# A hybrid attention and expert-lookup layer: the query-key product of each attention head contracts over 64 partitions instead of 128

## The chip, the core and the metric

The kernel runs as one program on one core of a Trainium2 chip. The metric is the device time of one execution in microseconds (us), taken as the median of several runs. All arithmetic is in float32.

## The reference, cut to what matters

One layer processes a prompt of 1024 tokens and a decoding sample of 64 tokens. A projection feeds two groups of heads, A and B. Then come an output projection, an expert lookup and a small gated tail:

```python
a = rmsnorm(h, norm_mix); z = a @ w_in
# group A: 4 heads x 128, gated DeltaNet in chunks. group B: 8 heads x 64, forgetting attention
s = einsum('bqhd,bkhd->bhqk', q, k) * 64 ** -0.5           # DH_B = 64
s = s + c_q[..., None] - c[:, :, None, :]                  # c: running sum of log f, per head
s = where(pos_q[:, None] >= pos_k[None, :], s, -inf)
o = einsum('bhqk,bkhd->bqhd', softmax(s), v)
h = h + concat(A, B) @ w_out
# expert lookup: 8 heads pick 16 of 16384 experts each, so 128 rows of u and 128 rows of v per token
h = h + sum_k softmax(score)_k * gelu(u[e_k] . x) * v[e_k]
```

Only the first product of the attention, queries times keys, is what the change touches.

## The kernel before, in words

**Tiles and steps.** The 1024 prompt tokens are nine tiles with the sample: tiles 0 to 7 of 128 tokens, and the sample as tile 8 (`LAST`). The program is 12 steps. Step `s` runs the front of tile `s` (projections, convolution, DeltaNet, attention, output projection, choice of experts), the u rows of tile `s-1`, the v rows of the tiles `s-2` and `s-3`, and the tail of tile `s-3`. Steps 1 and on have 68 slots. `plan_front` (L130) writes by hand which stage has a part in which slot; every engine walks the same plan in the same order (`walker`, L466), so the order on each engine is fixed, and only semaphores tie the engines together.

**Expert rows.** From slot 4 on each slot has two u rows and two v rows. Every row is one indirect DMA of 128 x 1024 floats (512 KB) that POOL issues (L674) into a ring of 10 buffers. A u buffer is used up by a dot product on DVE (L1664). A v buffer is used up by TensorE (`weighted`, L1204, matmul L1218): the stationary operand has 32 columns and goes to a 32-partition stripe of the output bank, so two tokens use different column stripes. POOL issues into a buffer only when its last user has signalled `consumed`.

**Attention.** In tile `i` a head sees `blocks_of(i)` blocks of 128 keys: i+1 of them for the prompt, two for the sample. Up to four blocks (512 columns) are one half, so tiles 0 to 3 and 8 have one half per head and tiles 4 to 7 have two. `fox_s` (L1129, slots 22 to 38) makes one half of the scores in `BB[0]` with two matmuls that accumulate: L1141, queries times keys, and L1142, which adds the running sums of log f (stationary `faux`, moving `aux`, both 128 partitions, mostly zeros). DVE then reduces the half with its mask (L1510) and frees the bank; ScalarE takes the exponential (L853); `fox_o` (L1146) transposes the probabilities (L1155) and multiplies them with the values (L1166). Between these stand the matmuls of the DeltaNet's triangular inverse (L1071, L1078, L1080) and the L1218 of the slot.

**Where the 64 partitions are.** The query projection leaves two heads per 128 partitions: head 2m on partitions 0 to 63, head 2m+1 on 64 to 127. ScalarE writes each head into its own `[128, 128]` slice of `fqT` (L773), on the partitions that it came on. The other 64 partitions of the slice are zeros from one memset at the start (L552). `kTc[:, h // 2, :]` holds the keys of both heads of a pair, on the same partitions. So L1141 contracts over 128 partitions, and the zeros of the queries drop the neighbour's keys.

**Records.** The trace shows a float32 matmul as two records, each a weight load (LDWEIGHTS, PEld) and a MATMUL (PE). A form such as `128*32` is the stationary operand's partitions times its columns.

Of the kernel before, what the change touches and what calls it, by code (L numbers as in the profile page):

```python
# [17 lines left out]
HA, HB, DHB = 4, 8, 64  # L18
# [57 lines left out]
def halves_of(i):  # L76
    return -(-blocks_of(i) // 4)
# [199 lines left out]
def build(nc, t, out):  # L277
    ctx = ExitStack()
    with ctx:
        def sb(name, shape, dt=F32):  # L280
            return ctx.enter_context(nc.sbuf_tensor(name, shape, dt))
# [36 lines left out]
        fqT = sb("fqT", [P, HB, P])  # L318
        kTc = sb("kTc", [P, HB // 2, SEQ])
# [79 lines left out]
        BB = [psum(f"bbank{g}", 512) for g in range(2)]  # L399
# [12 lines left out]
        def till(name, i, v=None):  # L412

            return S[name], at(name, i, v)
# [27 lines left out]
        def wait_out(eng, i, *pieces):  # L442

            for name in pieces:
                wait_piece(eng, PIECE_NO[i, name])
# [15 lines left out]
        def halves(i):  # L461

            n = blocks_of(i)
            return [range(4 * g, min(4 * g + 4, n)) for g in range(halves_of(i))]
# [112 lines left out]
        with nc.Block() as block:  # L577
# [348 lines left out]
            def _(pe):  # L926
# [202 lines left out]
                def fox_s(i, h):  # L1129
                    if h == 0:  # L1130
                        wait_out(pe, i, "fox_q0", "fox_q1")
                        pe.wait_ge(*till("aux_ready", i))
                    for g, own in enumerate(halves(i)):
                        m = halves_of(i) * h + g
                        if m == 0:
                            pe.wait_ge(*till("kT_done", i))
                        else:
                            pe.wait_ge(*till("s_red", i, m))
                        c = slice(P * own[0], P * own[-1] + P)
                        w = P * len(own)  # L1140
                        pe.matmul(BB[0][:, 0:w], fqT[:, h, :], kTc[:, h // 2, c], start=True, stop=False)  # L1141
                        pe.matmul(BB[0][:, 0:w], faux[:, h, :], aux[:, c], start=False, stop=True)\  # L1142
                            .then_inc(S["s_mm"], 1)
                        yield
# [84 lines left out]
                stages.update({f"conv{g}": (lambda i, g=g: conv(i, g)) for g in range(3)})  # L1229
                stages.update({f"inv{l}": (lambda i, l=l: inverse(i, l)) for l in range(LEVELS)})  # L1230
                stages.update({f"fox_s{h}": (lambda i, h=h: fox_s(i, h)) for h in range(HB)})
                stages.update({f"fox_o{h}": (lambda i, h=h: fox_o(i, h)) for h in range(HB)})
                stages.update({f"out{j}": (lambda i, j=j: out_proj(i, j)) for j in range(4)})
# [508 lines left out]
```

## Time and profile before

| | |
|---|---|
| median of 3 runs | 4056.99 us (4051.64 to 4060.16) |
| the profiled execution | 4062.07 us, span 4060.1 us |
| mean granted clock of TensorE | 0.874 of full speed |
| PE / DVE / POOL busy | 72% / 64% / 51% of the span |
| DMA | 1463 MB, 360 GB/s over the span |

The profiled execution is 2 us longer than its span, and 5 us longer than the median. Busy time of PE is modelled at its ends, so a busy PE is not PE at its peak; differences between start times are exact, and the text works with these.

### The profile page before, as it was taken

How to read it: one execution, taken by the hardware profiler on the slowest of the kernel's cores; microseconds unless marked ns; L12 is line 12 of the kernel's file. 1: busy time of each engine (PE TensorE's matmuls, PEld its weight loads, DVE VectorE, ACT ScalarE, POOL GpSimd, SP SyncE). 2: the span in 40 equal slices, each digit the busy share in tenths (PEclk: the TensorE clock that was granted, in tenths of full speed). 3: DMA queues.
4: the chain of work that ended last, by engine and by line, in shares of the span. 5: the costliest groups of instructions: out<-in, count | busy, mean ns of one | idle time of the engine just before them, and what ended most of it. 6: DMA issues, size and time to landing. Idle time of an engine off the chain costs nothing.

```text
span 4060.1 us, 42281 instructions
## 1 busy us (share of the span) xinstructions
PE 2913.4 (72%) x15157; PEld 1720.8 (42%) x15157; DVE 2582.4 (64%) x6198; ACT 564.5 (14%) x1106; POOL 2089.7 (51%) x2206
## 2 busy tenths in 40 slices
PE   6656627875887578876887589758885587566587
PEld 5656524443543354444545355435443353232122
DVE  3388885668666966687576856686564856495411
ACT  2112111101210021101110122012210121001000
POOL 0014435664566555755565546645563456546763
PEclk9778768987998899987999799879997799788899
DMA  6159959998999999999999999999999899999996
GB/s 200 54 215 369 349 206 412 410 410 339 413 411 410 372 383 412 406 404 351 413 388 413 349 413 375 403 346 411 390 343 326 325 413 409 350 346 399 410 407 262
DMA packets 390527, 1463.24 MB, mean 360 GB/s; under 512 B 64816, under 2 KB 67824, under 8 KB 355760
## 3 DMA queue, kind: packets, MB, share of 16 engines
q0 software_dynamic: 313344, 1140.99, 72.6%
q1 hardware_dynamic: 72112, 301.98, 18.9%
q10 hardware_dynamic: 4864, 17.57, 1.1%
q8 instruction: 122, 2.00, 0.2%
q14 instruction: 85, 0.70, 0.0%
HBM read 1446.15 MB, written 13.97 MB: 360 GB/s over the span
## 4 chain that ended last, share of the span: by engine, by line
PE 29%; DMA 28%; DVE 22%; POOL 11%; issue 8%; ACT 2%; DVEq 0%; ACTq 0%; POOLq 0%
DMA ring<-peer_v,idxT 23%; PE ybank L1218 11%; POOL ring L674 11%; DVE ring L1664 7%; PE abank L951 5%; PE abank L955 5%; DMA ring<-peer_u,idx 4%; DVE arena L1567 1%; DVE arena L1575 1%; DVE arena L1569 1%; DVE arena L1572 1%; DVE arena L1564 1%; PE bbank L1141 1%; PE bbank L1142 1%; PE bbank L1166 1%
## 5 line engine op out<-in xcount | busy, mean ns | idle before, releaser
L674 POOL DMA_INDIRECT ring<-peer_u,idx x1088 | 1038.2, 954 | 1374.9 <-PE ybank L1218 696.7
L1218 PE MATMUL ybank<-ring,vst 128*32 128x512 f32 x4352 | 1205.3, 688 | 612.1 <-DMA ring<-peer_v,idxT 598.4
L1664 DVE CUSTOM_DVE_ANT_0 ring<-ring,xn 128x1024 f32<-128x1024 f32 x1088 | 1298.9, 1217 | 504.7 <-DMA ring<-peer_u,idx 493.7
L674 POOL DMA_INDIRECT ring<-peer_v,idxT x1088 | 1042.6, 958 | 546.0 <-issue 258.7
L1218 PEld LDWEIGHTS ybank<-ring,vst 128*32 128x32 f32 x4352 | 251.0, 118 | 1288.4 <-issue 1280.8
L951 PEld LDWEIGHTS abank<-aT,wring 128*128 128x128 f32 x4608 | 544.9, 198 | 169.6 <-issue 154.3
L951 PE MATMUL abank<-aT,wring 128*128 128x128 f32 x4608 | 568.4, 284 | 63.3 <-issue 49.5
L955 PE MATMUL abank<-wring,aT 128*128 128x256 f32 (+1 forms) x1440 | 344.0, 396 | 12.2 <-DVEq L1326 6.8
L955 PEld LDWEIGHTS abank<-wring,aT 128*128 128x128 f32 x1440 | 278.2, 198 | 105.4 <-issue 60.0
L699 ACT ACTIVATE arena<-abank 128x256 f32<-128x256 f32 (+1 forms) x180 | 68.8, 383 | 1172.6 <-PE abank L951 898.5
L973 PE MATMUL bbank<-ident,arena 128*128 128x128 f32 x9 | 4.3, 474 | 246.8 <-DVE arena L1625 246.8
L955 PE MATMUL abank<-wring,arena 128*128 128x256 f32 (+2 forms) x648 | 173.8, 421 | 0.8 <-DVE arena L1270 0.8
L1653 DVE TENSOR_TENSOR vst<-wT,unit 128x128 f32<-128x128 f32 (+1 forms) x288 | 81.0, 282 | 123.2 <-PE ybank L1218 120.2
L955 PEld LDWEIGHTS abank<-wring,arena 128*128 128x128 f32 (+1 forms) x648 | 120.2, 192 | 57.4 <-issue 39.5
L1510 DVE CUSTOM_DVE_ANT_0 arena<-bbank,causal 128x512 f32<-128x512 f32 (+3 forms) x104 | 56.7, 545 | 125.7 <-PE bbank L1142 125.3
L1564 DVE MAX8 arena<-arena 128x8 f32<-128x128 f32 (+1 forms) x216 | 62.0, 328 | 111.1 <-ACT arena L891 108.9
L973 PEld LDWEIGHTS bbank<-ident,arena 128*128 128x128 f32 x9 | 1.6, 181 | 255.7 <-DVE arena L1625 255.7
L1664 DVE DVE_READ_ACCUMULATOR2_ANT dots<- 128x1 f32 x1088 | 89.1, 82 | 0.0
L1166 PEld LDWEIGHTS bbank<-vc,arena 128*128 128x128 f32 x608 | 74.7, 194 | 33.3 <-issue 25.9
L1141 PE MATMUL bbank<-kTc,fqT 128*128 128x512 f32 (+3 forms) x208 | 85.2, 492 | 0.6 <-DVE fst L1510 0.6
L1166 PE MATMUL bbank<-vc,arena 128*128 128x64 f32 x608 | 81.0, 278 | 5.2 <-ACT arena L862 5.2
L1142 PE MATMUL bbank<-aux,arena 128*128 128x512 f32 (+3 forms) x208 | 83.2, 482 | 0.0
(268 smaller groups left out, 2697.4 us busy)
## 6 DMA issues: line engine op xcount, KB each, us to landing
wring<-w_pieces SPq DMA_DIRECT2D x252, 1024.0 KB, 8.1
wring<-w_pieces SPq DMA_DIRECT2D x18, 1056.0 KB, 8.3
ring<-peer_u,idx POOLq DMA_INDIRECT x1088, 9.2
ring<-peer_v,idxT POOLq DMA_INDIRECT x1088, 9.3
wring<-w_pieces SPq DMA_DIRECT2D x18, 512.0 KB, 6.8
h_rows<-x ACTq DMA_DIRECT2D x8, 512.0 KB, 9.4
h<-h_rows ACTq DMA_DIRECT2D x8, 512.0 KB, 6.9
out_y_prompt<-arena ACTq DMA_DIRECT2D x8, 512.0 KB, 9.3
```

What stands on the lines that cost most here:

```text
L674: pool.indirect_dma_start(out=ring[:, r, :], out_offset=None, in_=t["peer_" + kind], in_offset=bass.IndirectOffsetOnAxis(ap=where, axis=0) ...
L699: last = act.activation(dst, src, func, scale=scale)
L951: last = pe.matmul(b[:, m * P:m * P + rows], wt[:, k, m * P:(m + 1) * P], actT[:, k, 0:rows], start=(k == 0), stop=(k == DK - 1))
L955: last = pe.matmul(b[0:rows, 0:w], actT[:, k, 0:rows], wt[:, k, :], start=(k == 0), stop=(k == k8 - 1))
L1141: pe.matmul(BB[0][:, 0:w], fqT[:, h, :], kTc[:, h // 2, c], start=True, stop=False)
L1142: pe.matmul(BB[0][:, 0:w], faux[:, h, :], aux[:, c], start=False, stop=True)\
L1166: last = pe.matmul(BB[1][:, 0:DHB], pts[:, m, :], vc[:, m, h * DHB:(h + 1) * DHB], start=(m == 0), stop=(m == n - 1))
L1218: last = pe.matmul(YB[g][QUAD * j:QUAD * j + QUAD, :], vst[:, slot, j, :], ring[:, r, 512 * g:512 * g + 512], start=(n // q == 0), stop=(n ...
L1510: v.tensor_tensor_reduce(out=pbuf[h % 2][:, c], in0=BB[0][:, 0:w], in1=mask, scale=1.0, scalar=NEG * 10, op0=ALU.add, op1=ALU.max, accum_o ...
L1564: last = v.max(vals[:, 0:8], values)
L1653: v.tensor_tensor(vst[:, n % VST, 0:q, :], bcast(columns, QUAD), over(unit[:, QUAD - 1 - m:2 * QUAD - 1 - m], q), ALU.mult)\
L1664: v.tensor_tensor_reduce(out=ring[:, r, :], in0=ring[:, r, :], in1=XN[:], scale=1.0, scalar=0.0, op0=ALU.mult, op1=ALU.add, accum_out=dots ...
```

## The change

The slice of partitions of head `h` is taken from both operands of L1141. The slice of an even head is 0 to 63, that of an odd head 64 to 127. The number of columns, the output, the accumulation with L1142, the semaphores and the memset of `fqT` stay as they are.

```diff
                         w = P * len(own)
-                        pe.matmul(BB[0][:, 0:w], fqT[:, h, :], kTc[:, h // 2, c], start=True, stop=False)
+                        o = DHB * (h % 2)
+                        pe.matmul(BB[0][:, 0:w], fqT[o:o + DHB, h, :], kTc[o:o + DHB, h // 2, c], start=True, stop=False)
                         pe.matmul(BB[0][:, 0:w], faux[:, h, :], aux[:, c], start=False, stop=True)\
```

## Rows read from the trace of the kernel before

**Rows 1.** The page: the span, and the chain that ended last by engine and line.
```profile
span 4060.1 us, 42281 instructions
PE 29%; DMA 28%; DVE 22%; POOL 11%; issue 8%; ACT 2%; DVEq 0%; ACTq 0%; POOLq 0%
DMA ring<-peer_v,idxT 23%; PE ybank L1218 11%; POOL ring L674 11%; DVE ring L1664 7%; PE abank L951 5%; PE abank L955 5%; DMA ring<-peer_u,idx 4%; DVE arena L1567 1%; DVE arena L1575 1%; DVE arena L1569 1%; DVE arena L1572 1%; DVE arena L1564 1%; PE bbank L1141 1%; PE bbank L1142 1%; PE bbank L1166 1%
```

**Rows 2.** Attention stages of tiles 0, 3, 4, 7: busy time, granted clock, DMA.
```profile
core 0: us, PE busy (x) PEld busy (x) DVE busy (x) ACT busy (x) POOL busy (x), PEclk, DMA share, GB/s
70.00:171.00 101.00, 67.55 (x397) 60.68 (x395) 41.02 (x95) 26.48 (x65) 0.00 (x0) 0.80 0.19 68
...
1142.00:1225.00 83.00, 73.46 (x380) 37.38 (x378) 56.82 (x112) 14.96 (x33) 57.94 (x61) 0.96 1.03 410
1572.00:1665.00 93.00, 82.08 (x453) 44.79 (x451) 65.51 (x148) 19.28 (x44) 61.89 (x67) 0.98 1.02 405
...
2877.00:2978.00 101.00, 95.00 (x488) 51.47 (x486) 62.54 (x134) 21.86 (x40) 59.42 (x64) 0.97 0.96 362
```

**Rows 3.** Chain of waits by line, stages of tiles 0, 4, 5, 6, 7, 8.
```profile
by line: PE abank L1071 8.5%; PE abank L951 7.3%; PE abank L1080 7.2%; PE abank L1078 7.0%; issue 4.8%; DVE arena L1424 3.8%; PE abank L955 3.4%; PE bbank L1166 3.1%; PE bbank L1141 2.5%; PE bbank L1142 2.4%; PE abank L1089 2.1%; PE abank L
...
by line: DMA ring<-peer_v,idxT 30.6%; PE ybank L1218 27.3%; POOL ring L674 10.1%; PE bbank L1141 6.8%; PE bbank L1142 6.7%; PE bbank L1166 6.0%; PE abank L1080 5.0%; PE abank L1071 4.7%; PE abank L1078 4.7%; issue 4.7%; PE bbank L1155 4.2%;
...
by line: DMA ring<-peer_v,idxT 29.2%; PE ybank L1218 28.5%; PE bbank L1166 8.4%; PE bbank L1141 8.0%; PE bbank L1142 8.0%; PE bbank L1155 5.4%; POOL ring L674 5.4%; PE abank L1080 4.8%; PE abank L1078 4.5%; PE abank L1071 4.5%; issue 3.4%; 
...
by line: DMA ring<-peer_v,idxT 29.1%; PE ybank L1218 26.0%; PE bbank L1166 9.6%; PE bbank L1141 9.1%; PE bbank L1142 9.1%; PE bbank L1155 5.9%; PE abank L1080 4.7%; PE abank L1078 4.4%; PE abank L1071 4.4%; POOL ring L674 2.8%; issue 2.5%; 
...
by line: PE ybank L1218 29.1%; DMA ring<-peer_v,idxT 18.3%; PE bbank L1141 12.8%; PE bbank L1142 12.8%; PE bbank L1166 10.8%; PE abank L1071 7.3%; PE bbank L1155 6.9%; PE abank L1080 5.5%; PE abank L1078 5.4%; ACT arena L868 1.4%; issue 1.1
...
by line: DMA ring<-peer_v,idxT 72.7%; POOL ring L674 21.4%; PE ybank L1218 15.9%; issue 9.2%
```

**Rows 4.** Timeline of PE, tile 7: start, us, instructions, idle before in brackets.
```profile
2904.75 1.02 PE L1141 MATMUL bbank<-kTc,fqT 128*128 128x512 f32 x2
2905.61 1.02 PE L1142 MATMUL bbank<-aux,arena 128*128 128x512 f32 x2
2906.56 1.91 PE L1218 MATMUL ybank<-ring,vst 128*32 128x512 f32 x8
2908.40 1.16 PE L1071 MATMUL abank<-arena 128*128 128x128 f32 x8
2909.39 1.90 PE L1166 MATMUL bbank<-vc,arena 128*128 128x64 f32 x16
...
2916.81 1.06 PE L1080 MATMUL abank<-arena 128*128 128x128 f32 x8
2917.70 0.60 PE L1155 MATMUL bbank<-ident,arena 128*128 128x128 f32 x4
2918.14 1.02 PE L1141 MATMUL bbank<-kTc,fqT 128*128 128x512 f32 x2
```

**Rows 5.** Timeline of weight loads and their matmuls, tile 6.
```profile
2451.19 0.97 PEld L1078 LDWEIGHTS abank<-arena 128*128 128x128 f32 x8 [0.84 <-issue]
2451.20 1.16 PE L1078 MATMUL abank<-arena 128*128 128x128 f32 x8
2452.08 0.97 PEld L1080 LDWEIGHTS abank<-arena 128*128 128x128 f32 x8
2452.19 1.06 PE L1080 MATMUL abank<-arena 128*128 128x128 f32 x8
```

**Rows 6.** Timeline, stationary operand of 64 partitions, in the tail of tile 8.
```profile
4027.79 0.46 PE L929 MATMUL bbank<-ident,arena 64*128 64x64 f32 x4 [3.69 <-DVE arena L1256]
```

**Rows 7.** Timeline of PE, tiles 2 and 3.
```profile
766.40 1.91 PE L1218 MATMUL ybank<-ring,vst 128*32 128x512 f32 x8 [0.57 <-DMA ring<-peer_v,idxT]
...
1179.94 1.02 PE L1141 MATMUL bbank<-kTc,fqT 128*128 128x512 f32 x2
...
1190.28 1.02 PE L1141 MATMUL bbank<-kTc,fqT 128*128 128x512 f32 x2
```

## The prediction

> **What bounds the kernel now.** I read the page first, then the stages of attention by windows, then the chain of waits inside each, then the timeline of PE. The page's chain is mixed: PE 29%, DMA 28%, DVE 22%, with L1141 and L1142 at 1% each [rows 1]. Such an average can't price an edit in one stage, so I went to the windows. In the stage of tile 3 the DMA moves 410 GB/s, in that of tile 4 it moves 405, but in that of tile 7 only 362, while PE is busy 95.0 of 101 us at a clock of 0.97 [rows 2]. The chain says the same by stage. From tile 4 to tile 7 the lines of PE take over: L1141 has 6.8%, 8.0%, 9.1% and 12.8% of it, and L1142 nearly the same; for the sample (tile 8) neither is in it, and DMA and POOL hold it [rows 3]. On the timeline of tile 7 PE runs one group behind the other with no wait on a landing [rows 4]. So the late tiles' attention is bound by PE, and what the change does to PE's order there goes into the time.
>
> **The change, part by part.** It removes 64 of the 128 partitions from both operands of L1141. It adds no instruction, wait or DMA, and moves none. The edit has three places of possible cost.
>
> *The matmul and its load.* The number of columns stays, and the time of a matmul goes by these: L1141 of 512 columns takes 2905.61 - 2904.75 = 0.86 us for its two records, 0.43 each [rows 4]. The one operand of 64 partitions in this trace gives no sign of a faster rate: four records of 64 columns take 0.46 us, where L1155's four of 128 columns take 0.60 [rows 4, 6]. That is 0.14 us less for 256 columns fewer, and at 0.86 / 1024 us a column it would be 0.21; the load ahead of the first, which is not hidden there, accounts for the rest. Value taken: 0. Bounds: 0, and a doubled rate, half of L1141's time.
>
> *The switch of shape.* This is the term that counts. Before, L1155 or L1080, L1141 and L1142 all have the form 128*128, and each one's first load runs beneath the matmul before it: the load of L1080 starts 0.11 us ahead of its matmul, while that of L1078, which follows the 128*32 matmuls of L1218, starts with its matmul, at 2451.19 and 2451.20 [rows 5]. So where the form changes, nothing is loaded ahead. The price can be read in tile 7. L1142 has the same work as L1141, but the L1218 behind it starts 2906.56 - 2905.61 = 0.95 us after it, not 0.86: 0.09 us of waiting until the array is empty. The first group behind L1218 takes 2909.39 - 2908.40 = 0.99 us, and the same work of L1080 with no change ahead takes 2917.70 - 2916.81 = 0.89: 0.10 us for the load that is now bare [rows 4]. A change into a form with 128 stationary columns thus costs 0.09 + 0.10 = 0.19, near 0.195 us. Afterwards L1141 is 64*128 between 128*128 groups, which makes two changes, one ahead of L1141 and one ahead of L1142: 0.39 us per half of a head. The change that L1218 brings behind L1142 was there before. The trace has no change between 64 and 128 partitions back to back (the L929 of rows 6 had stood idle), so this is an estimate from changes in columns. Bounds: 0 if partitions don't count as a form, and 0.35 us each, 0.70 per half, if each change showed the load of 0.19 us and the 0.16 by which a record of L1141 (1.02 - 0.43 = 0.59 us) outlasts its 0.43 us of columns [rows 4]. I take 0.39, since it is read off groups that stand next to L1141.
>
> The Trainium skill, "TensorEngine Tiling (Array Packing)", Tiling Modes, Key Properties, says that a change of tiling mode, and not only of tile, drains TensorE, and it counts 64 rows as a mode of its own. The 0.09 us of rows 4 agree for columns; no row shows it for rows of the array. The skill's "TensorE: Matmul & The Clock Gate", Part 2, gives the drain as about 128 cycles; at 2.4 GHz that is an estimate of 0.05 us where the trace has 0.09, and 2 x (0.05 + 0.10) = 0.31 us per half would make the sum below 21 instead of 26 us.
>
> *DVE and the bank.* L1510 waits for L1142's signal, which now comes up to 0.39 us later. DVE has queued behind it the dot products (L1664), and POOL waits for those. In the late tiles PE is late itself and DVE is busy 62.54 of 101 us, so DVE only waits longer [rows 2]. Cost of its own: 0. Without that cover it would be the 0.39 us that is already counted, not a second one.
>
> **What lies on the path.** The chain's share of L1141 counts the halves: tile 7 has 12.8% of 101 us = 12.9 us, at 0.86 each 15 halves. Tiles 6, 5 and 4 have 9.1% of 99, 8.0% of 97 and 6.8% of 93 us, which is 9.0, 7.8 and 6.3 us [rows 3]. Their two halves have 512 columns, and 384, 256 and 128; at 0.86 us per 512 the means are 0.75, 0.65 and 0.54 us, so 12, 12 and 12 halves. Together 51 of 64; the first ones of tiles 4 to 6 lie beside a wait on a landing. 51 x 0.39 = 19.9 us.
>
> Tile 0 has no gathers (POOL 0.00, DMA 68 GB/s) [rows 2] and its chain holds L1141 for 2.5% of 101 = 2.5 us [rows 3], which is all 8 heads: 0.22 us for 128 columns (a quarter of 0.86) at 2.4 GHz for five and twice that at 1.2 GHz for three make 2.4, and the mean granted clock there is 0.80 [rows 2]. 5 x 0.39 + 3 x 0.78 = 4.3 us.
>
> Tile 3: from 1179.94 to 1190.28 a head takes 10.34 us and PE waits on no landing [rows 7], while DMA is at its most, 410 GB/s [rows 2]. The two limits nearly coincide. I count five heads: 2.0 us; bounds 0 and 3.1 (eight heads). Tile 2: PE stands 0.57 us on a landing in each head [rows 7], more than 0.39, so it is hidden: 0. In tile 8 DMA and POOL hold the chain: 0. In tile 1, where L1141 is as small as in tile 0 and there are u rows only, I take 0 with 8 x 0.39 = 3.1 as the other bound.
>
> Sum: 19.9 + 4.3 + 2.0 = 26.2 us. The ring has ten buffers whatever happens, so POOL can't catch up later what PE's late release cost it: no give-back. On the profiled execution that is 4062.1 + 26.2 = 4088.3 us; that execution lies 5.1 us above the median, so the forecast is 4057 + 26 = 4083 us.
>
> **Rivals.**
>
> *A: partitions are no form (not slower).* The array keeps loading ahead over the change from 64 to 128 partitions, and L1141 costs what it did. It decides at one place, the load ahead of L1142 in tile 7: if that still starts under L1141, the price is 0 and the time stays at 4057. For it: the changes that the trace shows back to back are all in columns. Against it: where L1078 follows L1218, the new form takes in what the old one used and more, and its load starts late [rows 5]; L1142 stands to L1141 in the same way.
>
> *B: half the partitions are streamed faster.* The Trainium skill's "TensorEngine Tiling (Array Packing)", Overview, Theoretical Speedup, gives up to 2x for a small dimension of 64 or less. As a mechanism here the two records of L1141 would run beside each other, as those of two tokens do in L1218 (eight records in 1.84 us) [rows 4]. L1141 holds 12.9 + 9.0 + 7.8 + 6.3 = 36 us of the chain; half is 18, and with no cost of switching the time is 4039; with the switches it is 4057 + 26 - 18 = 4065. Against it: rows 6, and both records have the same partitions.
>
> *C: the change costs, but lies beside the DMA.* If the landings really pace tiles 4 to 7, only tile 0 pays: 4061. Against it: 362 GB/s in tile 7 where 410 can be had [rows 2].
>
> *D: only one of the two changes is bare,* for instance into the smaller form at once: half of 26, so 4070.
>
> *E: each change costs 0.35 us.* The 51 halves, five heads of tile 3 and five of tile 0 pay 0.70 and three of tile 0 at half the clock twice that: 61 x 0.70 + 3 x 1.4 = 47 us, so 4104. Against it: rows 4 show 0.19 for the nearest change.
>
> **How the numbers follow.** The forecast (two changes near 0.2 us each, paid where PE is late) has 0.60, with a range of its own of 4071 to 4095. D has 0.12, A 0.10, C 0.05, E 0.09, B 0.04. The range of 8 in 10 reaches from 4060 to 4102: it leaves out A, most of B, and half of E. About 0.2% (8 us) is what a measurement of this kernel can tell from no change. Faster by more: B without the cost of switching, 0.03. Within: A, C and the rest of B, 0.17. Slower: 0.80.
>
> **What would show it.** Right: L1141 has the form 64*128, its own 0.86 us for 512 columns stay, and L1141 to L1142 is about 1.05 us in tile 7, with the first loads of both groups starting with their matmuls; a head of tile 7 takes 13.4 + 0.8 = 14.2 us and DMA falls below its 362 GB/s there; tiles 2 and 8 stay. Wrong: the load of L1142 starts under L1141 (A), L1141's groups shrink (B), or the bare changes are there and the head of tile 7 is no longer (C).

## The result, and the profile after

The changed kernel takes 4087.37 us in the median of 4 runs (4083.69 to 4097.09), against 4055.67 us before. The ratio is 1.0076, with a 95% interval of 1.0055 to 1.0096: 22 to 39 us slower, 32 in the middle. The forecast was 26 us slower, 4083 us. The profiled execution took 4083.69 us, span 4082.0, 22 us above that of before.

The page of the changed kernel, with the lines that answer to [rows 1]:

```profile
span 4082.0 us, 42281 instructions
PE 30%; DMA 26%; DVE 23%; POOL 11%; issue 7%; ACT 2%; DVEq 0%; ACTq 0%; POOLq 0%
```

PE and DVE have a point more of the chain, DMA has two fewer and issue one fewer. That is all the page tells. L1141 is now L1142, and the lines behind it are one further down too. The timeline of weight loads (PEld) and matmuls (PE) in tile 7 answers to [rows 4] and [rows 5]:

```profile
2937.12 0.29 PEld L1142 LDWEIGHTS bbank<-kTc,fqT 64*128 64x128 f32 x2 [0.17 <-issue]
2937.12 1.12 PE L1142 MATMUL bbank<-kTc,fqT 64*128 64x512 f32 x2
2938.17 0.30 PEld L1143 LDWEIGHTS bbank<-aux,arena 128*128 128x128 f32 x2 [0.76 <-issue]
2938.17 1.12 PE L1143 MATMUL bbank<-aux,arena 128*128 128x512 f32 x2
2939.23 0.14 PEld L1219 LDWEIGHTS ybank<-ring,vst 128*32 128x32 f32 x4 [0.76 <-issue]
2939.23 1.91 PE L1219 MATMUL ybank<-ring,vst 128*32 128x512 f32 x8
...
2942.85 0.47 PEld L1156 LDWEIGHTS bbank<-ident,arena 128*128 128x128 f32 x4
2942.96 0.60 PE L1156 MATMUL bbank<-ident,arena 128*128 128x128 f32 x4
2943.49 0.29 PEld L1142 LDWEIGHTS bbank<-kTc,fqT 64*128 64x128 f32 x2 [0.17 <-issue]
2943.49 1.12 PE L1142 MATMUL bbank<-kTc,fqT 64*128 64x512 f32 x2
```

Three things are to be seen. The groups of both score matmuls begin their load and their matmul at the same time, 2937.12 and 2938.17, where L1156 (behind L1080, at 2942.85) still loads 0.11 us ahead. From L1142 to L1143 it is 1.05 us, and from L1143 to L1219 1.06; before, the same two distances were 0.86 and 0.95 [rows 4]. And four transposes ahead of L1142 take 2943.49 - 2942.96 = 0.53 us, not 0.44. So the added time of a half is 0.09 (emptying ahead of L1142) + 0.19 (its bare load, and emptying behind it) + 0.11 (the bare load of L1143) = 0.39 us.

The windows of the changed kernel over the attention of tiles 0 and 1 (columns as in [rows 2]) hold what the forecast did not have:

```profile
98.00:146.00 48.00, 38.96 (x170) 33.69 (x170) 12.04 (x36) 12.71 (x35) 0.00 (x0) 0.66 0.00 1
370.00:423.00 53.00, 42.45 (x204) 33.45 (x205) 48.27 (x98) 12.63 (x34) 27.11 (x29) 0.76 0.93 349
```

and the windows of the kernel before, for the same tiles:

```profile
98.00:146.00 48.00, 34.86 (x195) 30.75 (x193) 14.76 (x43) 14.29 (x41) 0.00 (x0) 0.78 0.00 1
370.00:420.00 50.00, 34.42 (x219) 29.80 (x218) 48.72 (x102) 11.34 (x37) 27.11 (x30) 0.91 0.95 357
```

The granted clock is 0.66 instead of 0.78 in tile 0, and 0.76 instead of 0.91 in tile 1.

By start times of the first matmul of each head, one of the heads in the middle of a tile, where the times repeat, takes, in us:

| tile | before | after | difference |
|---|---|---|---|
| 2 | 10.23 | 10.22 | 0 |
| 3 | 10.34 | 10.73 | 0.39, one half |
| 4 | 11.12 | 11.90 | 0.78, two halves |
| 5 | 11.87 | 12.65 | 0.78 |
| 6 | 12.63 | 13.41 | 0.78 |
| 7 | 13.39 | 14.17 | 0.78 |

### The profile page after: what moved, and what is told of

It is laid out like the page before. It is cut to its first block, busy times and chain, and to the rows that moved or that the text cites. A ratio compares the mean times of both kernels' runs of the same rounds, so it can differ in the third digit from the quotient of the medians.

```text
span 4082.0 us, 42281 instructions
## 1 busy us (share of the span) xinstructions
PE 2957.4 (72%) x15157; PEld 1721.4 (42%) x15157; DVE 2582.3 (63%) x6198; ACT 565.4 (14%) x1106; POOL 2097.2 (51%) x2206
## 4 chain that ended last, share of the span: by engine, by line
PE 30%; DMA 26%; DVE 23%; POOL 11%; issue 7%; ACT 2%; DVEq 0%; ACTq 0%; POOLq 0%
DMA ring<-peer_v,idxT 22%; POOL ring L674 11%; PE ybank L1219 10%; DVE ring L1665 7%; PE abank L951 5%; PE abank L955 4%; DMA ring<-peer_u,idx 3%; DVE arena L1568 2%; DVE arena L1576 2%; DVE arena L1570 2%; DVE arena L1573 1%; PE bbank L1143 1%; PE bbank L1142 1%; DVE arena L1565 1%; PE bbank L1167 1%
## 5 line engine op out<-in xcount | busy, mean ns | idle before, releaser
L1219 PE MATMUL ybank<-ring,vst 128*32 128x512 f32 x4352 | 1206.2, 688 | 598.6 <-DMA ring<-peer_v,idxT 587.8
L1219 PEld LDWEIGHTS ybank<-ring,vst 128*32 128x32 f32 x4352 | 250.8, 118 | 1272.5 <-issue 1264.9
L1143 PE MATMUL bbank<-aux,arena 128*128 128x512 f32 (+3 forms) x208 | 96.2, 546 | 0.0
L1142 PE MATMUL bbank<-kTc,fqT 64*128 64x512 f32 (+3 forms) x208 | 96.2, 544 | 0.0
```

The lines of the kernel that those rows point to most:

```text
L1142: pe.matmul(BB[0][:, 0:w], fqT[o:o + DHB, h, :], kTc[o:o + DHB, h // 2, c], start=True, stop=False)
L1219: last = pe.matmul(YB[g][QUAD * j:QUAD * j + QUAD, :], vst[:, slot, j, :], ring[:, r, 512 * g:512 * g + 512], start=(n // q == 0), stop=(n ...
```

## The experiments

Theory F (form): a change of the stationary operand's form costs PE 0.195 us, and nothing else is slower. Rival M (matmul): the matmul over 64 partitions is itself slower. A border is a place where one group of matmuls follows another, and an added change is a border whose two forms are the same before and differ after. The diffs of the experiments are against the changed kernel, unless said otherwise. Ratios are to the kernel before, whose median was 4057 to 4060 us beside the experiments.

### Again

The changed kernel, unchanged.

> The changed kernel as it is, timed beside the others of this call. Theory F (form): every change of the stationary operand's form (128*128, 64*128, 128*32) costs PE 0.09 us of emptying and a bare load of 0.10 us, and nothing else is slower; two more changes in each half of a head. Theory M (matmul): the matmul over 64 partitions is itself slower by 0.39 us, whatever stands beside it. Both expect what one profile has shown: 26 to 32 us above the kernel before, a head of tile 7 at 14.17 us (before 13.39), of tile 3 at 10.73 (before 10.34), of tile 2 unchanged. A third question is tile 0: its attention stretch was 8 us longer at a lower granted clock (0.66, before 0.79). If that is the change's doing it comes again; if it is where the clock happened to stand, it does not.

Measured: 4091.66 us, 35 us above the kernel before (4056.8) in that comparison, ratio 1.0085 (1.0072 to 1.0099), so 29 to 40 us. The heads of tiles 3 to 7 take the same as in the table to 0.01 us. Tile 0's stretch, from the start of its first score record to that of its last, is 46.1 us (46.2 in the first profile of the change), at a clock of 0.66 again. The kernel before has 38.1 us. The profiles of the kernels below that leave tile 0 as it was have 37.8 to 40.3 us, at a clock of 0.75 to 0.78, so the low clock and the longer stretch come with the change, and the stretch grows by 6 to 8 us.

### The other order of the two matmuls

```diff
-pe.matmul(BB[0][:, 0:w], fqT[o:o + DHB, h, :], kTc[o:o + DHB, h // 2, c], start=True, stop=False)
-pe.matmul(BB[0][:, 0:w], faux[:, h, :], aux[:, c], start=False, stop=True)\
+pe.matmul(BB[0][:, 0:w], faux[:, h, :], aux[:, c], start=True, stop=False)
+pe.matmul(BB[0][:, 0:w], fqT[o:o + DHB, h, :], kTc[o:o + DHB, h // 2, c], start=False, stop=True)\
```

> The changed kernel with the two matmuls of a half in the other order: the one with the running sums (128 partitions) first, queries times keys (64 partitions) second. F: one of the two added changes goes wherever the 128*32 matmuls follow, since that border was a change of form before too; a head of tile 7 takes 13.39 + 2 x 0.195 = 13.8 us, and the time is about 13 to 18 us above the kernel before (halves followed by a 128*128 group, in tile 0, 1 and the last ones, still pay two). M: nothing moves, 14.17 us a head and 26 to 32 us in all.

Measured: 4077.37 us, ratio 1.0051 (1.0035 to 1.0068), 21 us above the kernel before (14 to 28), the middle a little above the 13 to 18 expected. A head of tile 7 takes 13.78 us, as expected. Its timeline of PE, in tile 7:

```profile
2914.14 0.60 PE L1156 MATMUL bbank<-ident,arena 128*128 128x128 f32 x4
2914.58 1.02 PE L1142 MATMUL bbank<-aux,arena 128*128 128x512 f32 x2
2915.53 1.12 PE L1143 MATMUL bbank<-kTc,fqT 64*128 64x512 f32 x2
2916.59 1.91 PE L1219 MATMUL ybank<-ring,vst 128*32 128x512 f32 x8
```

L1156 to L1142 is 0.44 us as before the change, since nothing changes there. M is out: the same 64-partition matmul stands in every half, and half of the price of a head (0.39 of 0.78 us) has gone with one border.

### Only the even heads, with one matmul over 64 partitions, and with both

```diff
-o = DHB * (h % 2)
-pe.matmul(BB[0][:, 0:w], fqT[o:o + DHB, h, :], kTc[o:o + DHB, h // 2, c], start=True, stop=False)
-pe.matmul(BB[0][:, 0:w], faux[:, h, :], aux[:, c], start=False, stop=True)\
+o = slice(0, DHB) if h % 2 == 0 else slice(0, P)
+pe.matmul(BB[0][:, 0:w], fqT[o, h, :], kTc[o, h // 2, c], start=True, stop=False)
+pe.matmul(BB[0][:, 0:w], faux[o, h, :], aux[o, c], start=False, stop=True)\
```

That is the second kernel; the first leaves `faux[:, h, :], aux[:, c]` in the last line.

> Only the even heads contract over 64 partitions (0 to 63), the odd heads over 128 as before. F and M both expect half of the loss, 13 to 16 us; a pair of neighbouring heads of tile 7 takes 26.78 + 0.78 = 27.6 us. It is the base for the next kernel, and shows whether the two halves of the partitions cost the same. Where only 4 of tile 0's 8 heads are cut, its stretch should lose about 4 of the 8 us.

> As the kernel with the even heads alone, and in the even heads the matmul with the running sums contracts over partitions 0 to 63 too (its rows that are not zero lie there), so that both groups of a half have the form 64*128. There are now twice as many 64-partition matmuls as with the even heads alone, but half as many added changes. F: a pair of neighbouring heads of tile 7 takes 26.78 + 2 x 0.195 = 27.2 us, and the whole loss is about 6 to 8 us. M: 26.78 + 1.56 = 28.3 us a pair, and 26 to 32 us in all.

Measured: 4072.61 us (1.0032 to 1.0065) with one, 16 us above the kernel before, and 4067.25 us (1.0018 to 1.0039) with both, 10 us above it (7 to 16), where F expected 6 to 8 and M 26 to 32. A pair of heads of tile 7 takes 14.08 + 13.49 = 27.57 and 13.68 + 13.49 = 27.17 us. The timeline of the second, an odd head's half (128 partitions) and an even head's:

```profile
2906.17 1.02 PE L1142 MATMUL bbank<-kTc,fqT 128*128 128x512 f32 x2
2907.03 1.02 PE L1143 MATMUL bbank<-aux,arena 128*128 128x512 f32 x2
2907.98 1.91 PE L1219 MATMUL ybank<-ring,vst 128*32 128x512 f32 x8
...
2912.24 1.12 PE L1142 MATMUL bbank<-kTc,fqT 64*128 64x512 f32 x2
2913.20 1.02 PE L1143 MATMUL bbank<-aux,arena 64*128 64x512 f32 x2
2914.15 1.91 PE L1219 MATMUL ybank<-ring,vst 128*32 128x512 f32 x8
```

Between two groups of 64*128 nothing is emptied: L1142 takes 0.96 = 0.86 + 0.10 for its own bare load, and L1143 to L1219 takes the 0.95 that it took before the change: 512 columns over 64 partitions take the same time as over 128. In tile 7 twice as many 64-partition matmuls with half the added changes cost a pair of heads 0.39 us instead of 0.79. That is F.

### Where it is paid: tiles 4 to 7, tiles 0 and 1, tiles 2, 3 and 8

```diff
-o = DHB * (h % 2)
-pe.matmul(BB[0][:, 0:w], fqT[o:o + DHB, h, :], kTc[o:o + DHB, h // 2, c], start=True, stop=False)
+o = slice(DHB * (h % 2), DHB * (h % 2) + DHB) if 4 <= i < LAST else slice(0, P)
+pe.matmul(BB[0][:, 0:w], fqT[o, h, :], kTc[o, h // 2, c], start=True, stop=False)
```

The other two kernels have `i < 2` and `i in (2, 3, LAST)` in place of `4 <= i < LAST`.

> Only tiles 4 to 7 contract over 64 partitions, all other tiles over 128 as before. The forecast's sum has 51 halves x 0.39 = 19.9 us here, and the two profiles of the full change had 18 us by the lengths of the stretches: 4073 to 4077 us. If the loss came from the first tiles, or if the landings paced the late tiles, it would be under 8 us, 4065 or less. In the profile: a head of tile 7 at 14.17 us, of tile 3 at 10.34, tile 0 as before.

> Only tiles 0 and 1 contract over 64 partitions. The forecast's sum has 4.3 us here (tile 0) and 0 for tile 1: 4061 us. The rival, that a lower granted clock in these thinly filled stretches comes with the change, takes the two profiles at their word: 8.1 us in tile 0 and 5.7 in tile 1, so about 4070 us, at a clock of 0.66 in tile 0's attention (before 0.79) and 0.76 in tile 1's (before 0.93).

> Only tiles 2, 3 and 8 contract over 64 partitions. By the forecast tiles 2 and 8 hide it behind the landings, and tile 3 pays 0.39 us in about five heads: 2 us, 4059 us, not told from no change. If a change of form had a price that the landings don't hide, 24 halves would cost 9 us: 4066. In the profile: a head of tile 2 at 10.2 us as before, of tile 3 at 10.73.

Measured, beside 4059.09 us before:

| cut in | us | ratio (interval) | forecast |
|---|---|---|---|
| tiles 4 to 7 | 4080.13, +21 | 1.0052 (1.0035 to 1.0069) | +19.9 |
| tiles 0, 1 | 4070.33, +11 | 1.0026 (1.0017 to 1.0036) | +4.3 |
| tiles 2, 3, 8 | 4056.51, -3 | 0.9997 (0.9986 to 1.0008) | +2.0 |

The three add up to 30 us, near the whole. For tiles 0 and 1 it is the rival of that run's expectation (a lower clock that comes with the change, about 4070 us) that came true, not the forecast. Where the landings pace the kernel the price vanishes, and one can watch it vanish. Tile 2 of the changed kernel, on the timeline:

```profile
770.46 0.91 PE L1142 MATMUL bbank<-kTc,fqT 64*128 64x384 f32 x2
771.29 0.91 PE L1143 MATMUL bbank<-aux,arena 128*128 128x384 f32 x2
...
776.85 1.91 PE L1219 MATMUL ybank<-ring,vst 128*32 128x512 f32 x8 [0.17 <-DMA ring<-peer_v,idxT]
778.69 1.16 PE L1078 MATMUL abank<-arena 128*128 128x128 f32 x8
779.68 1.06 PE L1080 MATMUL abank<-arena 128*128 128x128 f32 x8
780.67 0.91 PE L1142 MATMUL bbank<-kTc,fqT 64*128 64x384 f32 x2
```

PE's wait for the v row was 0.57 us [rows 7] and is 0.17: the 0.39 came out of the wait, and the head still takes 10.21.

### What lowers the clock in tile 0

Against the kernel before: 128 partitions everywhere, and one small matmul of another form between the two, in tiles 0 and 1.

```diff
 pe.matmul(BB[0][:, 0:w], fqT[:, h, :], kTc[:, h // 2, c], start=True, stop=False)
+if i < 2:
+    pe.matmul(YB[0][0:QUAD, 0:1], ones[:, 0:QUAD], ones[:, 0:1], start=True, stop=True)
 pe.matmul(BB[0][:, 0:w], faux[:, h, :], aux[:, c], start=False, stop=True)\
```

> The kernel before, 128 partitions everywhere, but in tiles 0 and 1 one more matmul stands between the two of each half: stationary ones of 128 partitions x 32 columns, one moving column, into an output bank that is idle there and whose content is not used. It makes two changes of form per half, as the change does, and no matmul over 64 partitions. It asks what lowers the granted clock in the thin tiles. If the emptied array does (theory E), tile 0's attention stretch gets about 8 us longer (38 to 40 us before, 46 with the change) at a clock near 0.66, tile 1's about 4 to 6, and the time is near 4070. If the halved partitions do (theory H), only the direct price is paid, some 0.45 us in each of 8 heads, so 42 to 43 us at a clock of 0.75 or more, and the time is 4060 to 4063.

Measured: 4063.72 us beside 4059.85, ratio 1.0008 (0.9999 to 1.0018), which is 4 us more (0 to 7). The windows of this kernel, tiles 0 and 1:

```profile
98.00:146.00 48.00, 38.14 (x177) 33.75 (x177) 12.64 (x36) 12.43 (x34) 0.00 (x0) 0.64 0.00 1
374.00:420.00 46.00, 33.94 (x216) 27.48 (x214) 44.79 (x92) 11.02 (x31) 24.73 (x27) 0.93 0.97 364
```

Tile 0's stretch is 47.2 us, a little longer than with the change, at the same low clock, with no matmul over 64 partitions in it. What the clock costs there is seen on the timeline of the same kernel:

```profile
102.72 0.27 PE L1143 MATMUL ybank<-ones 128*32 128x1 f32 x2
102.92 0.79 PE L1144 MATMUL bbank<-aux,arena 128*128 128x128 f32 x2
103.50 1.92 PE L1078 MATMUL abank<-arena 128*128 128x128 f32 x8
105.21 1.75 PE L1080 MATMUL abank<-arena 128*128 128x128 f32 x8
```

and of the kernel before:

```profile
102.69 1.21 PE L1078 MATMUL abank<-arena 128*128 128x128 f32 x8
103.73 1.06 PE L1080 MATMUL abank<-arena 128*128 128x128 f32 x8
```

L1078 and L1080 of eight records take 1.92 and 1.75 us, at 1.2 GHz (the granted clock from 103.5 to 106.7 us is 0.51); before, they take 1.21 and 1.06, nearly all at 2.4 GHz (1.00 from 103.0 to 104.6). So in tile 0 two added changes of form per half are enough to bring the lower clock (theory E of the expectation), and the halved partitions (theory H) are not needed for it. A small matmul of the neighbours' form, which would add an instruction and no change of form, was not run.

In tile 1 it is not so: its clock stays at 0.93 and its stretch at 46.4 us here (46.0 before), but they are 0.76 and 51.7 us with the change. The small matmul with one moving column is not the same load as the change, and what tells the two apart in tile 1 is open. Nor does the number of added changes fix the clock: the two kernels with the even heads alone both add eight in tile 0, and their stretches are 42.6 us at a clock of 0.71 and 39.9 us at 0.75; in tile 1 it is the other way round, 46.4 and 49.2 us.

The time is below the 4070 us expected with E, and just above the 4060 to 4063 expected with H. E had a longer tile 1 in it, which did not come, so the time is not evidence for either; the stretch and the clock of tile 0 are.

### Fewer changes of form: the v rows of two slots together

F prices something that was there all along: the matmuls of the v rows are 128*32 and stand in every slot between 128*128 groups. Against the kernel before, four tokens in every second slot instead of two in each:

```diff
-                    _step[_slot + _j // 2].append(("v", _t, _from + _j))
+                    _step[_slot + 2 * (_j // 4) + 1].append(("v", _t, _from + _j))
```

> The kernel before (128 partitions everywhere), with the v rows of two slots brought together in the second of them: four tokens per group of 128*32 matmuls instead of two, so half as many changes into and out of that form, and four column stripes in use at a time instead of two. Follows from theory F, by which each group of the v rows pays the same price of form. If the four stripes run beside each other, 16 records take about as long as 8 did (1.84 us): a head of tile 7 loses one such group and goes from 13.39 to about 11.5 us, tiles 4 to 6 from 11.12, 11.87 and 12.63 towards the 10.2 us that the landings allow. At most 8 heads x (0.9 + 1.6 + 2.0 + 1.9) = 51 us, some 30 to 50 us gained: 4005 to 4027. The rival: v rows that are used in bunches of four hold their buffers of the ten longer, so POOL waits and the stretches that the landings pace get longer; then the gain is under 10 us, or a loss.

Measured: 4153.24 us, ratio 1.0252 (1.0229 to 1.0276), 94 us slower, where 30 to 50 us of gain were expected. The mechanism works on PE: 16 records take as long as 8 did, and a head of tile 7 takes 11.46 us. But the rival decides the time. The waits of the two kernels, before and then this one (engine, line, releaser: us in total, times, longest):

```profile
PE ybank L1218 <- DMA ring<-peer_v,idxT: 598.4, 311, 8.4
```

```profile
PE ybank L1218 <- DMA ring<-peer_v,idxT: 1048.0, 199, 14.5
```

PE waits 450 us more for v rows. A likely reason is that a buffer that waits for its fourth token isn't free for the next row, so that the DMA runs dry where it sets the pace; POOL's wait on L1218 also grew, from 727 to 817 us. The mean granted clock fell too, from 0.88 to 0.79, and how much of the 94 us each of the two makes was not separated. From the first to the last score matmul the attention of tiles 4 to 7 was 1, 10, 8 and 16 us shorter, tiles 0 and 1 stayed as they were, and from there on the other attention stretches and all the stages between them were longer. So the next two kernels do it only there.

```diff
-                    _step[_slot + _j // 2].append(("v", _t, _from + _j))
+                    _at = _slot + _j // 2
+                    if 5 <= _s < 8 and 24 <= _at < 40 and _at % 2 == 0:
+                        _at += 1
+                    _step[_at].append(("v", _t, _from + _j))
```

The other has `4 <= _s < 8 and 22 <= _at < 42`.

> The kernel before with the v rows brought together by two slots only where PE sets the pace: in steps 4 to 7, slots 22 to 41. With it everywhere the four stretches were 1, 10, 8 and 16 us shorter, 36 us in all, and all the rest was longer. If these gains stand alone, and entering and leaving the stretch costs a few us each, the time is 4025 to 4045, and a head of tile 7 takes 11.5 us. The rival: what was lost elsewhere comes in on either side of each stretch, because the ring is emptier when the projections begin; then 4055 or more.

> As the last, but only in steps 5 to 7 and slots 24 to 39, that is without tile 4, where PE and the landings are nearly even, and with two slots less at each end. Gains of 10, 8 and 16 us at the most: 4028 to 4045 if tile 4 gave nothing in the last kernel, and below it if the ends of the stretch are what costs.

Measured, beside 4059.85 us before: 4052.48 us with the wider range, ratio 0.9985 (0.9976 to 0.9994), and 4043.53 us with the narrower, ratio 0.9959 (0.9947 to 0.9972), within its 4028 to 4045. The narrower one beats both kernels: 16 us (11 to 22) under the one before, and 44 under the changed one in its first measurement. The timeline of PE in it, tile 7:

```profile
2902.64 1.02 PE L1144 MATMUL bbank<-kTc,fqT 128*128 128x512 f32 x2
2903.50 1.02 PE L1145 MATMUL bbank<-aux,arena 128*128 128x512 f32 x2
2904.45 1.93 PE L1221 MATMUL ybank<-ring,vst 128*32 128x512 f32 x16
2906.31 1.16 PE L1081 MATMUL abank<-arena 128*128 128x128 f32 x8
...
2909.49 1.02 PE L1145 MATMUL bbank<-aux,arena 128*128 128x512 f32 x2
2910.35 1.15 PE L1074 MATMUL abank<-arena 128*128 128x128 f32 x8
...
2914.10 1.02 PE L1144 MATMUL bbank<-kTc,fqT 128*128 128x512 f32 x2
```

L1221 runs 16 records in 1.86 us, and L1145 to L1074 is 0.86 us: a border without a change. A head takes 11.46 us instead of 13.39. The three stretches are 8, 14 and 12 us shorter in the profile, 33 in all, of which the total keeps 16. The wider range did not reach the 4025 to 4045 us expected of it. In tile 4, where PE and the landings are nearly even, it gained nothing, and in its profile the first heads of tiles 4 to 7 took 17.8 to 19.0 us instead of 15.4 to 16.4. That tile 4, and not the two slots at each end, is the cause was not tried apart.

## Why the prediction was right

**The term that counts** was the price of a form, taken from changes in columns and carried over to partitions: 0.39 us per half. The trace after has 0.39, in its parts, and a head of tile 7 takes 14.17 us, where the forecast named 14.2 as its sign. The Trainium skill, "TensorEngine Tiling (Array Packing)", Tiling Modes, Key Properties, has it that changing the tiling mode drains TensorE and changing the tile alone doesn't. The trace agrees for rows of the array: 1.05 us between L1142 and L1143 with a change, 0.86 without. The estimate of 0.05 us of emptying, from the 128 cycles of the Trainium skill's "TensorE: Matmul & The Clock Gate", Part 2, is too low; the trace has 0.09 at either border, so the measurement decides.

**The matmul and its load**: no faster over 64 partitions. L1143 to L1219 takes 0.95 us with 64 partitions and with 128. Rival B is out.

**The path**: 19.9 us in tiles 4 to 7, measured 21 (14 to 28) with the cut there alone. The steady heads there pay the full 0.78, and the four stretches grew by 17 to 18 us in the profiles of the full change and of that cut, of the 64 x 0.39 = 25 us that would come without any cover; so the count of 51 halves was good to a few us. DMA fell from 362 to 347 GB/s in the stage of tile 7, as the forecast had it. The landings hide the price in tile 2, and tiles 2, 3 and 8 together are not told from no change; tile 3's heads did become 0.39 us longer, as the 2.0 us had it, but its 2 us can't be seen in the total. Rivals A, D and E are out by the 0.39 itself, and C by the cut in tiles 4 to 7.

**The mis-sized term** is "5 x 0.39 + 3 x 0.78 = 4.3 us" for tile 0, with 0 for tile 1. The two together cost 11 us (1.0017 to 1.0036, so 7 to 15). The sum took the clock of the profile before as given, and the change itself lowered it. The direct price was even a little less than the sum's. The first head of tile 0, at a granted clock of 0.50 (1.2 GHz) in both kernels, before and after:

```profile
99.93 2.07 PE L1071 MATMUL abank<-arena 128*128 128x128 f32 x8 [1.38 <-DVE arena L1424]
101.79 0.63 PE L1141 MATMUL bbank<-kTc,fqT 128*128 128x128 f32 x2
102.22 0.63 PE L1142 MATMUL bbank<-aux,arena 128*128 128x128 f32 x2
```

```profile
98.31 2.08 PE L1071 MATMUL abank<-arena 128*128 128x128 f32 x8 [1.38 <-DVE arena L1425]
100.31 0.79 PE L1142 MATMUL bbank<-kTc,fqT 64*128 64x128 f32 x2
101.04 0.79 PE L1143 MATMUL bbank<-aux,arena 128*128 128x128 f32 x2
101.62 1.91 PE L1078 MATMUL abank<-arena 128*128 128x128 f32 x8
```

From L1071 to L1078 it is 102.69 - 99.93 = 2.76 us before and 101.62 - 98.31 = 3.31 after, 0.55 us more and not the 0.78 that the sum took at the lower clock. Five heads at 0.39 and three at 0.55 make an estimate of 3.6 us, and the stretch grew by 6 to 8. The rest is laid to what the other matmuls lose to the lower clock, as L1078 does here: 1.91 us against 1.21. The small matmul between the two shows that added changes of form bring that clock there. For tile 1 the bound of 3.1 us was too tight (3.8 and 5.7 us longer in the profiles of the cut in tiles 0 and 1 and of the full change); its cause is open.

**How near the number came.** 26 us were forecast; 32 (22 to 39) and, in the second comparison, 35 (29 to 40) were measured, so the middle of the forecast was low, by about what tiles 0 and 1 cost beyond their 4.3 us. It stayed near because the late tiles are the larger part.

**The give-back.** The forecast held that nothing comes back. In the two profiles of the full change the lag behind the kernel before was 29 and 34 us at the end of tile 7's attention and 21 and 27 at the start of tile 8's, which looks like a give-back of 8 us. But the other profiles do not bear it out: with the cut in tiles 4 to 7 alone the lag stays at 18 us over the same stretch, and with the cut in tiles 2, 3 and 8, where tile 7 is as before, 9 us are gained there. So this stretch differs by up to 9 us between profiles, whether or not the late tiles are changed, and a give-back is not shown.

## What to carry to other kernels

In this kernel the zeros in the contraction cost TensorE nothing, since the neighbours have the full form; taking them out saves nothing and costs 0.39 us (at 2.4 GHz) wherever the smaller form stands between two groups of the larger one. Count the borders at which the stationary operand's form changes, not the partitions in use, and price a border only in stretches where the chain of waits runs through PE. A cheaper order in those stretches can be a loss in the ones that the landings pace, so restrict it to where it pays. And where PE is idle in part, as in tile 0 here, look at the granted clock as well: its loss was about as large as the price itself.

## What was not expected

- Sixteen added changes of form in tile 0's attention, an estimated 3.6 us in all with the change, went with a granted clock of 0.64 to 0.66 in all five profiles that have them, against 0.75 to 0.78 in the six that leave tile 0 as it was, and the lower clock cost about as much again.
- Four column stripes run in the time of two: 16 records of 512 columns in 1.86 us, 8 in 1.84.
- Bringing four tokens together cost 94 us where it was done in every step and gained 16 us where it was done in three.
